# The chunkwise delta-rule recurrence of one decoder layer: the state-free steps of both 64-token chunks of a tile taken together, 18 steps in place of 30

## What is computed

```python
def rwkv7_recurrence(r, w, k, v, kk, a):
    def step(S, inp):
        r_t, w_t, k_t, v_t, kk_t, a_t = inp
        sa = jnp.einsum('bhvk,bhk->bhv', S, -kk_t)
        S = (S * w_t[:, :, None, :] + sa[..., None] * (kk_t * a_t)[:, :, None, :]
             + v_t[..., None] * k_t[:, :, None, :])
        return S, jnp.einsum('bhvk,bhk->bhv', S, r_t)
...
def block(args):                      # the PEER feed-forward, 128 tokens at a time
    xb, ib, gb = args
    u = jnp.take(u_tab, ib, axis=0)
    coef = gb * jax.nn.gelu(jnp.einsum('cd,ced->ce', xb, u), approximate=False)
    return jnp.einsum('ce,ced->cd', coef, jnp.take(v_tab, ib, axis=0))
```

## Time and profile before

| | |
|---|---|
| time, median of 3 executions | 3565.68 us (3564.07 to 3578.39) |
| span of the profiled execution | 3574.8 us |
| PE busy | 2750.1 us (77%) |
| VectorE busy | 2366.9 us (66%) |
| GpSimd busy | 1971.4 us (55%) |
| ScalarE busy | 518.5 us (15%) |
| moved | 1246.47 MB, 1073.87 of them gathers |

### The profile page before, as it was taken

The page is one execution under the profiler, slowest core; times in us unless marked ns, Lnnn a source line. Parts: engine busy times, 40 slices in busy tenths (PEclk is TensorE's granted clock), DMA queues, the critical chain, the costliest instruction groups (busy, mean ns, idle before and its releaser), DMA issues.

```text
span 3574.8 us, 41985 instructions
## 1 busy us (share of the span) xinstructions
PE 2750.1 (77%) x15556; PEld 1281.8 (36%) x15556; DVE 2366.9 (66%) x6052; ACT 518.5 (15%) x1152; POOL 1971.4 (55%) x2093
## 2 busy tenths in 40 slices
PE   9899886888888789886856684667756777677787
PEld 7777762332323333332313332233323331122111
DVE  5678889676676667766677766767686757665200
ACT  3221311110111102011011101010111101111100
POOL 0014345555655566556665666656665666666663
PEclk9999997999999899997867887778767788788899
DMA  6558998999999999989999999999999999999996
GB/s 219 212 177 304 359 344 298 327 363 376 379 355 321 364 378 384 361 318 405 392 368 339 372 409 338 357 332 406 383 361 329 392 407 407 380 370 386 380 352 244
DMA packets 385293, 1246.47 MB, mean 349 GB/s; under 512 B 40512, under 2 KB 75072, under 8 KB 384320
## 3 DMA queue, kind: packets, MB, share of 16 engines
q0 software_dynamic: 294912, 1073.87, 79.5%
q1 hardware_dynamic: 90176, 169.91, 13.3%
HBM read 1216.75 MB, written 26.87 MB: 348 GB/s over the span
## 4 chain that ended last, share of the span: by engine, by line
PE 42%; DVE 17%; another core or an unknown queue 13%; DMA 11%; issue 11%; POOL 4%; ACT 2%; SPq 1%; POOLq 0%; DVEq 0%; ACTq 0%
PE e_acc L1324 12%; PE e_pl L1412 6%; DVE e_u L2240 5%; PE e_pd L1226 3%; PE e_pd L1200 3%; PE e_pd L1020 3%; PE e_acc L1369 3%; PE e_pd L1287 3%; PE e_acc L1394 2%; DMA e_u<-in_u_tab,e_idx 2%; DVE e_late L2240 2%; DMA e_late<-in_v_tab,e_idxT 2%; DMA e_v<-in_v_tab,e_idxT 2%; DMA e_v<-in_w_in 2%
## 5 line engine op out<-in xcount | busy, mean ns | idle before, releaser
L2240 DVE CUSTOM_DVE_ANT_0 e_u<-e_u,e_c 128x1024 f32<-128x1024 f32 x776 | 941.1, 1213 | 331.1 <-DMA e_u<-in_u_tab,e_idx 243.9
L985 POOL DMA_INDIRECT e_u<-in_u_tab,e_idx x776 | 746.5, 962 | 705.5 <-DVE e_dots L2240 283.5
L1324 PE MATMUL e_acc<-e_v,e_wd 128*32 128x512 f32 x2844 | 830.3, 703 | 189.2 <-DMA e_v<-in_v_tab,e_idxT 127.6
L993 POOL DMA_INDIRECT e_v<-in_v_tab,e_idxT x711 | 677.9, 953 | 497.9 <-PE e_acc L1324 222.1
L1412 PE MATMUL e_pl<-e_late,e_v 128*128 128x512 f32 x608 | 342.1, 660 | 60.0 <-DMA e_v<-in_w_in 13.5
L2240 DVE CUSTOM_DVE_ANT_0 e_late<-e_late,e_c 128x1024 f32<-128x1024 f32 x248 | 300.4, 1212 | 111.9 <-DMA e_late<-in_u_tab,e_idx 75.6
L1324 PE MATMUL e_acc<-e_late,e_wd 128*32 128x512 f32 x832 | 271.7, 714 | 95.3 <-DMA e_late<-in_v_tab,e_idxT 48.5
L985 POOL DMA_INDIRECT e_late<-in_u_tab,e_idx x248 | 239.8, 967 | 166.7 <-DVE e_dots L2240 113.1
L1324 PEld LDWEIGHTS e_acc<-e_v,e_wd 128*32 128x32 f32 x2844 | 115.4, 116 | 562.4 <-issue 294.5
L1963 DVE SCALAR_TENSOR_TENSOR e_gbc<-e_hc,e_cw,e_gbc 128x128 f32<-128x128 f32 x960 | 303.9, 343 | 0.4
L993 POOL DMA_INDIRECT e_late<-in_v_tab,e_idxT x208 | 197.8, 951 | 139.2 <-issue 54.4
(11 more groups left out here) (298 smaller groups left out, 3207.4 us busy)
## 6 DMA issues: line engine op xcount, KB each, us to landing
e_u<-in_w_in SPq DMA_DIRECT2D x38, 512.0 KB, 3.8
e_v<-in_w_in SPq DMA_DIRECT2D x38, 512.0 KB
e_v<-in_w_in SPq DMA_DIRECT2D x76, 256.0 KB
e_u<-in_u_tab,e_idx POOLq DMA_INDIRECT x776
e_zb<-in_w_c SPq DMA_DIRECT2D x48, 256.0 KB
e_v<-in_v_tab,e_idxT POOLq DMA_INDIRECT x711
e_arena<-in_w_r SPq DMA_DIRECT2D x32, 256.0 KB
e_zb<-in_w_r SPq DMA_DIRECT2D x32, 256.0 KB
```

The source lines that it names most:

```text
L985: pool.indirect_dma_start(out=rows_in[i], out_offset=None, in_=io["u_tab"], in_offset=bass.IndirectOffsetOnAxis(ap=idx[n % 2][:, j:j + 1], ...
L993: pool.indirect_dma_start(out=rows_in[i], out_offset=None, in_=io["v_tab"], in_offset=bass.IndirectOffsetOnAxis(ap=idxT[n % (LAG + 1)][:, ...
L1324: last = pe.matmul(acc[rows, cols], w[:, at_:at_ + 32], rows_in[row][:, cols], start=(step == 0), stop=True, skip_group_check=True)
L2240: dve.tensor_tensor_reduce(rows_in[i], rows_in[i], c[:, :], 1.0, 0.0, ALU.mult, ALU.add, dots[n % 2][:, j:j + 1]).then_inc(s_dot, 1)
```

## The change

The steps that do not need the state are done for both chunks of a tile at once. Each tile has 18 steps, step j at slot 20 + 5j//2 (20, 22, 25, 27, ... 62) instead of 30 at every third half slot (20, 21, 23, 24, ... 63).

- k = 0 and 1 are the first key-query products of chunk 0 and of chunk 1; k = 2 has the second ones of both: 32 matmuls.
- k = 3 to 11 are the inverse of both chunks: `squares` is now 16 matmuls, so that k = 3, 4, 5, 8, 9 have 32 and k = 6, 7, 10, 11 have 16. The copies and additions behind them are twice as wide (128x1024 or 128x512 on ACT, 128x512 on DVE), and half as many.
- The transposes move from k = 2 into k = 10 to 13, four to a step.
- k = 12, 13, 14 are the steps with the state for chunk 0, and k = 15, 16, 17 for chunk 1.
- The products are the same 376 matmuls and transposes for a tile. ACT has 24 parts for a tile instead of 30, DVE 17 instead of 26.
- `gs` of chunk 1 lies in `actT`; `bt` and `xs` have a copy for each chunk; `sq` and `yrstd` have places of their own.

```diff
-REC_PE, REC_ACT, REC_DVE = 16, 15, 13
+REC_PE, REC_ACT, REC_DVE = 20, 24, 17
...
-REC_AT, REC_STEPS = 20, 2 * (REC_PE - 1)
+REC_AT, REC_STEPS = 20, 18
...
-    j = -(-2 * (s - REC_AT) // 3)
-    return divmod(j, REC_PE - 1) if s >= REC_AT and j < REC_STEPS and REC_AT + 3 * j // 2 == s else None
+    j = -(-2 * (s - REC_AT) // 5)
+    return j if s >= REC_AT and j < REC_STEPS and REC_AT + 5 * j // 2 == s else None
...
                 def squares(out, a, b):
+                    for m in range(2 * PAIRS):
+                        for e in range(2):
+                            r = rows2[e]
+                            last = pe.matmul(pi[r, out, m * CH:(m + 1) * CH], a[r, m, :], b[r, m, :] if len(b.shape) == 3 else b[r, :],
+                                             start=True, stop=True)
+                    return last
...
+                if k == 2:
+                    pe.wait_ge(s_rv, n_v + 4)
+                    for which in range(2):
+                        for m in range(2 * PAIRS):
+                            for e in range(2):
+                                r, (ch, i) = rows2[e], divmod(m, PAIRS)
+                                lhs, rhs = (qv[ch][r, i, 0, :], bk[ch][r, i, e, :])[::1 - 2 * which]
+                                last = pe.matmul(pi[r, which, m * CH:(m + 1) * CH], lhs, rhs, start=True, stop=True)
+                if k == 3:
+                    pe.wait_ge(s_rv, n_v + 7)
+                    squares(0, d1[:, 1, :, :], d1[:, 0, :, :])
+                    last = squares(1, d1[:, 0, :, :], d1[:, 1, :, :])
...
+                if k == 5:
+                    pe.wait_ge(s_ra, n_a + 2)
+                    pe.wait_ge(s_rv, n_v + 8)
+                    squares(0, d2[:, 0, :, :], inv_z[:, :, :])
+                    last = squares(1, d1[:, 1, :, :], d1[:, 0, :, :])
...
                 if k in (3, 8):
-                    copied(both(d2), pi[:, :, 0:PAIRS * CH])
+                    copied(both(d2), pi[:, :, :])
...
-                if k in (0, 1, 5, 6, 7, 10):
+                if k in (0, 1, 2, 5, 6, 7, 10):
                     dve.wait_ge(s_rp, n_p + k + 1)
...
                 if k in (5, 6, 7):
-                    dve.wait_ge(s_rv, n_v + k + 1)
-                    dve.tensor_tensor(inv_z[:, :, :], grid(pi[:, int(k == 7), 0:small]), inv_z[:, :, :], ALU.add).then_inc(s_rv, 1)
+                    dve.wait_ge(s_rv, n_v + k + 3)
+                    dve.tensor_tensor(inv_z[:, :, :], grid(pi[:, int(k == 7), :]), inv_z[:, :, :], ALU.add).then_inc(s_rv, 1)
                 if k == 8:
-                    dve.wait_ge(s_ra, n_a + 7)
-                    dve.tensor_tensor(inv_f[:, :, :], d2[:, 1, :, :], mask(id2[:, :]), ALU.add).then_inc(s_rv, 1)
+                    dve.wait_ge(s_ra, n_a + 4)
+                    dve.tensor_tensor(inv_e[:, :, :], d2[:, 1, :, :], mask(id2[:, :]), ALU.add).then_inc(s_rv, 1)
```

More of the change, by code:

```diff
@@ L481, in trunk @@
         p_w, p_run, p_dec, p_a = (part(a, 4, "p (i t) -> p i t", i=PAIRS) for a in (14, 18, 22, 26))
-        sq, yrstd = (gs[:, e, :, :].rearrange("p i t -> p (i t)") for e in range(2))
+        sq, yrstd = (part(a, 4) for a in (14, 18))
         sc_ = buf("e_sc_", [P, PAIRS, HD])
@@ L490, in trunk @@
         mixt = actT
+        gs = [part(14, 8, "p (e i t) -> p e i t", e=2, i=PAIRS),
+              actT[:, :, :].rearrange("p k t -> p (k t)").rearrange("p (e i t) -> p e i t", e=2, i=PAIRS)]
         p_kk, p_nrm = actT[:, 0:PAIRS, :], actT[:, PAIRS:, :]
@@ L1083, in rec @@
-                if k == 12:
-                    if q:
-                        pe.wait_ge(s_ra, n_a)
-                    for i in range(PAIRS):
-                        for e in range(2):
-                            o = pi[rows2[e], 0, i * HD:(i + 1) * HD]
-                            pe.matmul(o, qv[:, i, 0, :], state[:, i, e, :], start=True, stop=False)
-                            last = pe.matmul(o, gs[:, e, i, 0:CH], xs[:, i, e, :], start=False, stop=True)
-                if k == 13:
-                    pe.wait_ge(s_ra, n_a + 10)
-                    last = squares(1, inv_e[:, :, :], rs[:, :, :])
@@ L1094, in rec, with outputs @@
-                if k == 14:
-                    pe.wait_ge(s_ra, n_a + 12)
-                    for i in range(PAIRS):
-                        pe.matmul(pi[:, 0, i * CH:(i + 1) * CH], state[:, i, :, :].rearrange("p e v -> p (e v)"), qv[:, i, 1, :],
+                            last = pe.matmul(pi[r, 1, i * CH:(i + 1) * CH], inv_e[r, ch * PAIRS + i, :], rs[r, i, :], start=True, stop=True)
+                    return last
+                def outputs(ch):
+                    for i in range(PAIRS):
+                        pe.matmul(pi[:, 0, i * CH:(i + 1) * CH], state[:, i, :, :].rearrange("p e v -> p (e v)"), qv[ch][:, i, 1, :],
@@ new lines, in rec @@
+                if k == 12:
+                    pe.wait_ge(s_ra, n_a + 9)
+                    right_side(0)
+                    last = pairs_turned(1, bk[1])
+                if k == 13:
+                    pe.wait_ge(s_ra, n_a + 11)
+                    solved(0)
+                    last = pairs_turned(0, vv[1])
+                if k == 14:
+                    pe.wait_ge(s_ra, n_a + 15)
+                    last = outputs(0)
+                if k == 15:
+                    pe.wait_ge(s_ra, n_a + 18)
+                    last = right_side(1)
@@ L1108, in rec @@
+                if k == 16:
+                    pe.wait_ge(s_ra, n_a + 19)
+                    last = solved(1)
+                if k == 17:
+                    pe.wait_ge(s_ra, n_a + 21)
+                    last = outputs(1)
                 last.then_inc(s_rp, 1)
@@ L1516, in square @@
+                if k in (12, 15):
+                    copied(flat(rs[:, :, :]), pi[:, 0, 0:PAIRS * HD])
+                if k == 12:
+                    key_side(1)
+                if k == 13:
+                    solved(0)
+                    value_side(1)
+                if k == 14:
+                    outputs(0)
+                if k == 16:
+                    solved(1)
+                if k == 17:
+                    outputs(1)
             def square(src, column, n, sem_src, s_dst):
```

271 lines of the change are left out of this document (137 added, 134 removed).

## The result

| | before | changed |
|---|---|---|
| time, median of 13 executions | 3564.18 us (3561.73 to 3578.39) | 3582.23 us (3570.59 to 3593.08) |
| span of the profiled execution | 3574.8 us | 3587.8 us |
| VectorE busy | 2366.9 us | 2356.2 us |
| ScalarE busy | 518.5 us | 507.8 us |

The ratio is 1.0037, with a 95% interval of 1.0025 to 1.0049. The forecast was 3490 us, the range 3435 to 3577.

A forecast was written before the change was run, and what follows sets the result against it. DVE's waits for the recurrence were taken to bound the late tiles; 65 us saved there plus 15 in the first tiles made 80, so 3495 against the profiled span, 3486 against the median, given as 3490 us (3435 to 3577).

The forecast's parts named there:

- What bounds the kernel: Late tiles t = 4 to 6: DVE waits for the recurrence, 46.8 us at t = 4; no engine fills the stretch.
- The amount of work: Per tile: wider instructions save DVE 1.4 us and ACT about 1 us; DVE's own work at t = 4 becomes 98.6.
- The size of E: For a step of 64 passes: between 5.8 and 9.2 us, middle 7.5 taken; late tiles save 65 us.
- E: Time from a PE step's first pass to its reader; mean of six before the change 4.6 us.
- The waits: DVE's waits for PE steps or copies, sixteen places a tile becoming ten: 28.5 us forecast at t = 4, against 46.8.
- The first tiles: t = 0 to 3 and the unhidden part: 5 us each at t = 2 and 3, 3 and 2 elsewhere, sum 15 us.
- Two rules weighed: Skill page's signal time, some 0.06 us against 5.4 late in the trace, and its warning of low clock after waits.
- The first: Rival: PE answers later, E near 10, late tiles save 27 us and first ones nothing, 3539 us; chance 0.19.
- The second: Rival: the gathers are the bound, so the change does nothing, 3555 to 3575 us; chance 0.12.
- The third: Rival: wide steps hold up token adds, POOL stands still, from E = 11.4; slower by 54 us, 3620; chance 0.14.
- W: Sum of DVE's waits in the t = 4 stretch, 5E − 9: 28.5 us forecast, 61 at E = 14.
- signs of being wrong: E outside 5.8 to 9.2, waits at covered steps, rate staying 340 GB/s without waits, or slots after 66 giving gains back.

The follow-up runs named there:

- the plain DMA: Kernel before with u rows fetched by plain DMA of consecutive table rows, not gathers: 3366.43 us against 3589.92 with late signals; changed kernel likewise, prompt signals: 3347.52 us.
- late groups: Groups of runs in which PE's signals came late; the unedited kernel before took 3590 and 3565 us in the two of them.
- the repeated pair: Both kernels run again without edit, signals late: changed kernel 3606.79 us, ratio 1.0045; kernel before 3579.0 us in one execution.
- prompt group: One of four groups of runs with PE's signals undelayed: unedited kernel before 3359 to 3361 us; changed kernel 3346.97 us in one, ratio 0.9965.

## Why the prediction was wrong

**What bounds the kernel.** Right: in the late tiles DVE's waits for the recurrence, 5.4 us unexplained after a step of 1.15 us, and not the gathers. That these waits are the bound was confirmed by the plain DMA: without them the stretch at t = 4 takes 118.4 us, at 408 GB/s.

**The amount of work.** Near: DVE's own work at t = 4 was forecast at 98.6 and is 99.4 us, so 0.6 us of the 1.4 were saved.

**The size of E.** Right for the large steps: forecast 7.5 us for a step of 64 passes, measured 7.1 in the mean of 18, with 14 of them between 5.8 and 9.2. Of the steps above the second takes 8.2 us to ACT's copy (1899.91 to 1908.12), the first 5.9 (1892.90 to 1898.83), and the mask of step 2 is taken up 9.0 us after its first pass (1881.93 to 1890.96). Wrong for the small ones, for which the forecast had 4.6 or less: 7.8 in the mean of nine.

**The step that failed is "The waits".** It says of steps 6, 7 and 10 "half as large (E now 4.6 or less) against three slots, 6.3 us: nothing", and gives "Steps 0 and 1: 1 us each" and "Steps 14 and 17 have ten and seven slots of cover: 1.4 each": 4.8 us in all. They cost 34.8 (L1904 7.0, L1908 9.1 + 8.3, L1933 5.7, and of L1927 1.1 for step 6 and 3.6 for step 7), while the large steps 2, 5 and 8, for which the forecast had 23.7 us, cost 16.3. The rows already spoke against it: the two longest waits in the earlier trace rows, 9.8 and 9.1 us at L1875, belong to k = 14, whose products are small. I forecast 1.4 each for their successors, and they became 9.1 and 8.3. I had taken the delay as a property of the step and cover as something that runs down at DVE's pace. The traces of the late groups show instead that PE stands still, or crawls at one to four passes every 0.7 to 1.4 us, while GpSimd issues gather on gather, and that GpSimd ends its chain only when rows run out. Cover then buys gathers, not time. A small step with ten slots of cover can then be as late as a large one.

**Why fewer steps did not help** can be argued from it, but no experiment shows it alone. PE has the same 15,556 passes to get through, and with late signals more of them cost more: 3,840 more took 133 us there, and 62 and 68 with prompt ones.

**The first tiles.** Forecast 15 us, 10 of them at t = 2 and 3 and next to nothing ahead of t = 0. In the two profiled executions it was the other way: 7.3 us were saved ahead of t = 0, 1.4 at t = 0 and 4.3 at t = 3, and t = 1 and 2 lost 1.1 and 1.7 (slots 20 to 66). The sum of about 10 us is near by luck; in the repeated pair it is a loss of 0.9.

**Two rules weighed.** In a prompt group L1020 from 1783.93 ends at 1786.01 (the profile models this end) and ACT starts at 1786.06, 0.05 us later; in the late groups the signal comes several us later. The Trainium skill, "TensorE: Matmul & The Clock Gate", section "The cost: per-tile semaphore tail", gives 0.06 us for one increment, an estimate by its formula. The prompt trace agrees, the late ones do not. The clock was hardly a cause: 0.78, 0.76 and 0.72 before, 0.74, 0.75 and 0.74 after.

**The rivals.** The first (PE answers later, E near 10) had a smaller saving, but not for the right reason: E was 7.1. Its thought that instructions come late is not refuted. The second (the change does nothing, 3555 to 3575) is nearest in the time, but the gathers are the bound in the prompt groups alone. The third is nearest in what it names, token adds held up behind a step and GpSimd standing still for want of a row; its condition, E over 11.4, was not met, and its price of 54 us was three times too high (by its own W of 61 the late tiles make 12.8, 9.0 and 10.9 us and not 13 each, so 48). Two of the signs of being wrong came true: the waits stand at steps held covered, and the slots after 66 lost time.

**What stays open.** Why slots 66 to 128 got longer, which is what made the kernel slower and not just equal, was not settled by an experiment. The repeated pair has it again at t = 3 to 6, by 14.5, 5.8, 2.6 and 2.6 us, but for the same kernel before these stretches differ between the two groups by up to 9 us. Nor is it known what makes a group late or prompt, or whether it is PE's supply of instructions or something else of PE that GpSimd's gathers hold up. The transfers that the profile lists as instructions do not show it: eight of 16 KB in the stretch at t = 4 of the changed kernel, of about 1 us each, in a late and in a prompt group alike, and none of them during the crawl of 1901.9 to 1907.6.

## What to carry to other kernels

When the reader of a result starts several us after the products have ended, don't size that delay by the step, and don't cover it with slots, before you know what ends it: look at which engine pauses just ahead of the late signal. Here the whole forecast gain of the late tiles hung on that. The cheapest test was to let the suspected engine do half of its transfers in another way; the cheapest remedy was a wait on it, placed where the signal is due, and it costs 0.4% where the signals are prompt. Look also where a gain lies, and not only at its size. And measure a small gain in more than one session: the same change was 0.4% slower in one and 0.35% faster in another.

## What the runs showed of the hardware

PE can be slowed while GpSimd issues indirect gathers one after another, whose rows the slowed products do not read: one to four passes every 0.7 to 1.4 us in a chain of six gathers, and the 21 long waits for its results at t = 4 to 6 ended 1.2 to 2.6 us after GpSimd's last issue. With every second gather a plain DMA of as many bytes, at 408 GB/s, nothing of it was left. This comes and goes between sessions, on a chip of the same number, and with it 6 to 7% of the kernel's time (3565 to 3590 us against 3360), at a granted clock of 0.85 to 0.87 over the span against 0.88 to 0.90.
